# Sixteen 32x32 products in the expert combine, and a new order around two norms and two projections

## The chip, the cores and the metric

The kernel runs on one core of one Trainium2 chip. The metric is device time in microseconds (us), median of several executions; lower is better. All arithmetic that counts is 4-byte floating point. Where the program wants the accuracy of full precision from the faster rounded form (fp32r), it splits both operands into a high and a low part and makes three matmuls of one product.

## The reference, cut to what matters

Two blocks on 512 tokens of width 1024. The change touches only the first:

```
mod = silu(c) @ w_ada + b_ada                  # 6 vectors of 1024: shift1, scale1, gate1, shift2, scale2, gate2
hn = rmsnorm(x, norm1_g) * (1 + scale1) + shift1
... = split(hn @ w_in)                         # heads of two attentions, gates ga, gb
merged = sigmoid(ga) * (ya @ w_proj_a) + sigmoid(gb) * (yb @ w_proj_b)
x = x + gate1 * (merged @ w_out)
hn2 = rmsnorm(x, norm2_g) * (1 + scale2) + shift2
qh = hn2 @ w_q ; s = qh . sub_keys             # 8 heads x 2 halves x 128 keys
eidx, g = the 16 best of 16 x 16 sums, softmax # 8 heads x 16 experts for each token
pre = hn2 . u[eidx] ; coef = g * gelu(pre)
f = sum over the 128 of coef * v[eidx]         # the combine
x = x + gate2 * f
```

The second block (attention with forget gates, pooling, a feed-forward of width 2816) follows; `u` and `v` are tables of 16384 rows of 1024.

## The kernel before, in words

Everything is written out by hand for each engine: the order of the work is the order of the code in the blocks `sync`, `tensor`, `scalar`, `vector` and `gpsimd`, and semaphores tie them together (`ready(n)` waits until n+1 events have been told, `free(n, depth)` until n+1-depth have). Activations lie transposed, channels on the partitions. A dense tile is 1024 input rows by 128 output columns of weights, 512 KB, and comes through a ring of four slots from SyncE's queue (`refill`, L623 and L662). ScalarE rounds it (`high`, L1323), VectorE takes the remainder (`low`, L1915), TensorE makes 8 x 3 matmuls of 512 columns (`product`, L688 to L690; `dense`) and the result goes to one of eight PSUM banks.

**The first norm.** SyncE loads `w_ada` in 48 tiles of 512 KB through six slots (L617): six, then `x` (2 MB), then ten more, then the first four weight tiles. VectorE makes one dot product for each (`ada_tile`, L1897). Tiles 0 to 7 are shift1, 8 to 15 scale1. When all sixteen are done it adds the bias (L1910), makes the gain, splits weight tile 0, and then goes over the eight channel tiles: `hn` (L1894), the rounded part on ScalarE (L1332), the low part `hn_low` (L1894). TensorE takes weight tile 0 as these come (a wait for each k in `dense`), and tile 1 after it.

**The projections.** After the attention, eight tiles of both `w_proj` (each 2 x 4 x 3 matmuls, ya first and yb second, one bank each: 0,1 and 2,3 in turn), then eight of `w_out` (banks 0 and 1). VectorE gates and adds each pair (L2079 to L2082), splits the sum (`merged_high`, `merged_low`), and tells `dense_dve`. TensorE waits for all of ya, yb and the gates before the first `w_proj` tile and for the last merged tile before the first `w_out` tile.

**The second norm and the queries.** The same as the first norm, with `w_q` tiles: `query(0)`, then `query(1)`, `key_scores(0)`, `query(2)`, `key_scores(1)`, `token_rows(0)`, and so on (L904 to L934). `choose(0)` on VectorE begins when the key scores of tiles 0 and 1 have been copied out, and ends with the first 16 expert numbers, which release GpSimd's first gather.

**Experts.** For each of 4 x 8 x 16 = 512 rows n, GpSimd issues an indirect DMA (`gather`, L1867) that brings, for each of 128 tokens, one row of u beside one row of v, 8 KB, 1 MB in all, into one of eight slots. VectorE multiplies the u half with the token's row (`dots`, L1897), ScalarE makes gelu and weight (L1512, L1518) and scales a folded unit matrix with it into `diag` (L1526), and TensorE adds the v halves (`combine`, L947), two rows at a time. A slot may be filled again when its combine has been made. Between the combines stand, by a fixed table of ticks, the remaining queries and the whole second block for the first half of the tokens (`block2(0)`); the second half (`block2(1)`) comes after the last combine.

The combine cuts the 128 tokens in two halves, so that four 64x64 quarters of the array are in use:

```
for a in range(2):
    for odd in range(2):
        s = (n + odd) % SLOT
        for t in range(2):
            k = slice(HALF * t, HALF * t + HALF)
            b = t ^ odd
            last = mm(bank(4 + 2 * odd + a)[HALF * b:HALF * b + HALF, :], diag[k, s, :],
                      rows[k, s, D + a * 512:D + (a + 1) * 512], start=c == 0, stop=c == P - 2)
```

Even rows n add into banks 4 and 5, odd ones into 6 and 7 with the halves crossed. `turn` brings both back to channels on partitions, with the unit matrix and with one whose halves are crossed (L963, L964).

## Time and profile before

| | |
|---|---|
| time, median of 3 runs | 2453.24 us (2450.24 to 2456.2) |
| the profiled execution's own time | 2461.37 us |
| its span in the profile | 2459.6 us |
[...]
| busy: PE, PEld, DVE, ACT, POOL | 84%, 50%, 58%, 41%, 24% |
| combine (L947): records, busy, mean | 4096, 632.0 us, 744 ns |
| gathers (L1867): issues; queue's bytes | 512; 542.25 MB |
| read from HBM | 707.56 MB, 289 GB/s over the span |

PE is TensorE's matmuls, PEld its weight loads, DVE VectorE, ACT ScalarE, POOL GpSimd, SP SyncE; SPq and DVEq are sequencers. A 4-byte (f32) product has two records in the trace, an fp32r one has one. Busy time of PE overlaps with itself, since matmuls are pipelined and their ends are modelled; the start of the next instruction is the better measure. "x16" is a count of records, and what stands in brackets is the idle time before and who ended it.

### The profile page before, as it was taken

The numbers are of one execution on the slowest core, as the hardware profiler recorded it, in microseconds if no ns is written. First come the engines' busy times: TensorE is split into PE (matmuls) and PEld (weight loads), VectorE is DVE, ScalarE is ACT, GpSimd is POOL, SyncE is SP. The second block draws the span as 40 slices with busy tenths as digits, with TensorE's granted clock in tenths as the row PEclk, the third lists the DMA queues.
The fourth block names the chain that finished last, engine by engine and source line by source line (L and its number), as shares of the span: only waits on it lengthen the run. The fifth ranks groups of instructions, "written<-read, shape, count | busy, mean of one in ns | idle before, by whom it ended". The sixth has DMA issues, their size and how long they took to land.

```text
span 2459.6 us, 29836 instructions
## 1 busy us (share of the span) xinstructions
PE 2063.2 (84%) x10672; PEld 1239.6 (50%) x10672; DVE 1427.6 (58%) x3242; ACT 1008.1 (41%) x2400; POOL 593.7 (24%) x570
## 2 busy tenths in 40 slices
PE   5999999999878765655656798889999987899999
PEld 3877557776534321111112363345666653677887
DVE  7742764453777677777777858774433433222554
ACT  3123435523434333333334566854444312353443
POOL 0000000000344444445444324433333331000000
PEclk9999999999988877878687899889999998999999
DMA  8821002132899999999999999999999997313655
GB/s 324 311 78 69 1 18 67 62 95 76 327 420 420 420 420 418 414 421 418 413 420 396 390 382 383 394 388 419 418 418 418 418 418 319 113 52 103 181 180 170
DMA packets 123585, 711.59 MB, mean 289 GB/s; under 512 B 14593, under 2 KB 15745, under 8 KB 57649
## 3 DMA queue, kind: packets, MB, share of 16 engines
q0 software_dynamic: 74608, 542.25, 53.7%
q1 hardware_dynamic: 48592, 167.33, 19.4%
q8 instruction: 81, 1.33, 0.2%
q14 instruction: 64, 0.52, 0.1%
q10 hardware_dynamic: 240, 0.16, 0.0%
HBM read 707.56 MB, written 2.13 MB: 289 GB/s over the span
## 4 chain that ended last, share of the span: by engine, by line
PE 57%; DMA 25%; DVE 7%; ACT 6%; issue 3%; POOL 2%; ACTq 0%; SPq 0%; DVEq 0%
DMA arena<-experts,eidx 24%; PE psum L947 10%; PE psum L688 8%; PE psum L689 8%; PE psum L690 8%; PE psum L1259 5%; DVE arena L1897 4%; POOL arena L1867 2%; PE psum L1237 2%; PE psum L1114 2%; PE psum L1064 2%; PE psum L800 1%; ACT sq L1526 1%; PE psum L776 1%; ACT arena L1518 1%
## 5 line engine op out<-in xcount | busy, mean ns | idle before, releaser
L947 PE MATMUL psum<-arena,sq 64*64 64x512 f32 x4096 | 632.0, 744 | 321.5 <-ACT sq L1526 311.8
L1897 DVE CUSTOM_DVE_ANT_0 arena<-arena 128x1024 f32<-128x1024 f32 x560 | 679.0, 1224 | 358.9 <-DMA arena<-experts,eidx 325.2
L1867 POOL DMA_INDIRECT arena<-experts,eidx x512 | 577.5, 1128 | 957.7 <-PE psum L947 773.7
L947 PEld LDWEIGHTS psum<-arena,sq 64*64 64x64 f32 x4096 | 153.8, 155 | 707.3 <-ACT sq L1526 472.3
L1512 ACT ACTIVATE arena<-arena 128x2 f32<-128x2 f32 x256 | 52.1, 203 | 718.1 <-DVE arena L1897 706.3
L688 PE MATMUL psum<-hn_high,w_high 128*128 128x512 f32 (+1 forms) x432 | 179.0, 414 | 14.7 <-DVE hn_low L1894 13.3
L689 PE MATMUL psum<-hn_low,w_high 128*128 128x512 f32 (+1 forms) x432 | 173.8, 402 | 0.0
L690 PE MATMUL psum<-hn_high,ring_low 128*128 128x512 f32 (+1 forms) x432 | 172.5, 399 | 0.0
L1259 PE MATMUL psum<-n_t,ring 128*128 128x256 f32 x704 | 161.7, 384 | 0.6 <-issue 0.6
L1526 ACT ACTIVATE sq<-sq,arena 128x64 f32<-128x64 f32 x512 | 150.3, 340 | 24.1 <-ACT arena L1518 0.4
L1259 PEld LDWEIGHTS psum<-n_t,ring 128*128 128x128 f32 x704 | 130.7, 190 | 45.7 <-issue 29.4
L1915 DVE TENSOR_TENSOR ring_low<-ring,w_high 128x1024 fp32r<-128x1024 f32 x74 | 90.4, 1224 | 77.2 <-ACT w_high L1323 70.7
L1323 ACT ACTIVATE w_high<-ring 128x1024 fp32r<-128x1024 f32 x74 | 77.6, 1052 | 133.6 <-PE psum L690 127.4
L2205 DVE TENSOR_TENSOR ring_low<-ring,last_high 128x1024 fp32r<-128x1024 f32 x66 | 80.7, 1225 | 82.9 <-ACT last_high L1550 82.2
L1518 ACT ACTIVATE arena<-arena 128x1 f32<-128x1 f32 x512 | 122.9, 287 | 10.6 <-ACT arena L1512 0.4
L688 PEld LDWEIGHTS psum<-hn_high,w_high 128*128 128x128 f32 (+1 forms) x432 | 82.2, 190 | 60.5 <-issue 33.8
L1550 ACT ACTIVATE last_high<-ring 128x1024 fp32r<-128x1024 f32 x66 | 69.8, 1060 | 82.1 <-DMA ring<-w_stream 82.1
L1512 ACT ACT_TABLE_LOAD x75 | 96.2, 1283 | 6.0 <-ACT hn_rest L1785 3.7
L690 PEld LDWEIGHTS psum<-hn_high,ring_low 128*128 128x128 f32 (+1 forms) x432 | 82.3, 190 | 20.1
L689 PEld LDWEIGHTS psum<-hn_low,w_high 128*128 128x128 f32 (+1 forms) x432 | 82.6, 191 | 17.4
L1856 POOL TENSOR_SCALAR_AFFINE_SELECT arena<-arena 128x128 f32<-128x128 f32 x32 | 9.4, 295 | 272.0 <-DVE arena L1894 271.6
L688 PE MATMUL psum<-last_high,n_high 128*128 128x512 f32 (+1 forms) x192 | 72.6, 378 | 1.2 <-DVE n_low L2218 1.1
(316 smaller groups left out, 3150.5 us busy)
## 6 DMA issues: line engine op xcount, KB each, us to landing
ring<-w_stream SPq DMA_DIRECT2D x262, 512.0 KB
arena<-w_ada SPq DMA_DIRECT2D x48, 512.0 KB, 6.4
arena<-experts,eidx POOLq DMA_INDIRECT x512
arena<-cum_rows POOLq DMA_DIRECT2D x1, 2112.0 KB, 10.3
x<-xT SPq DMA_DIRECT2D x1, 2048.0 KB, 15.2
arena<-rel_rows POOLq DMA_DIRECT2D x1, 2048.0 KB, 15.2
arena<-sub_keys POOLq DMA_DIRECT2D x1, 1024.0 KB, 6.3
outT<-hn_rest SPq DMA_DIRECT2D x8, 128.0 KB, 10.1
```

The lines of the kernel that those rows point to most:

```text
L688: mm(out, a[0], b[0], start=start, stop=False)
L689: mm(out, a[0], b[1], start=False, stop=False)
L690: return mm(out, a[1], b[0], start=False, stop=stop)
L947: last = mm(bank(4 + 2 * odd + a)[HALF * b:HALF * b + HALF, :], diag[k, s, :], rows[k, s, D + a * 512:D + (a + 1) * 512], start=c == 0, st ...
L1259: last = mm(bank(b, PAIR), w[:, k, :], n_t[:, k, 0:PAIR], start=k == 0, stop=k == KT - 1)
L1512: steps(op(pre[:, s:s + 2], pre[:, s:s + 2], ACT.Gelu))
L1518: steps(op(coef[:, s + c:s + c + 1], pre[:, s + c:s + c + 1], ACT.Copy, scale=wgt[:, n // P % 2, k:k + 1]))
L1526: op(diag[:, s + c, :], ident_pair, ACT.Copy, scale=coef[:, s + c:s + c + 1]).then_inc(diag_done.sem, 1)
L1867: nc.gpsimd.indirect_dma_start(rows[:, s, :], None, experts, bass.IndirectOffsetOnAxis(ap=eidx[:, n // P % 2, n % P:n % P + 1], axis=0)).t ...
L1897: return V.tensor_tensor_reduce(out=out, in0=a, in1=b, scale=1.0, scalar=0.0 if op1 == ALU.add else -TAKEN, op0=op0, op1=op1, accum_out=accum)
L1915: V.tensor_tensor(ring_low[:, n % SLOTS, :], ring[:, n % SLOTS, :], rounded(n).bitcast(f32), ALU.subtract)\
L2205: V.tensor_tensor(ring_low[:, n % SLOTS, :], ring[:, n % SLOTS, :], last_high[:, n % SLOTS, :].bitcast(f32), ALU.subtract).then_inc(w_spli ...
```

## The change

1. **Combine.** The tokens are cut in quarters of 32. For each half a of the columns and each of two rows (odd), four products of 32x32x512 go to one bank, quarter t of the tokens to quarter t ^ (2*odd + a) of the partitions, so that the sixteen products of one combine use sixteen different 32x32 tiles. `diag` and the folded unit matrix become 32 wide, the latter made with three additions for one, and `turn` uses matrices that undo the crossing.
2. **First norm.** `w_ada` is loaded in the order scale1, shift1, the rest. SyncE issues three tiles, `x`, five tiles, weight tiles 0 and 1, eight tiles, weight tiles 2 and 3. VectorE makes the gain after eight tiles, and then for each k one more dot product, one bias addition of one column, `hn`, and `hn_low` of k-2, with the splits of weight tiles 0 and 1 at k = 1 and 2. A small step on the attention's bias rows moves behind the second product tile.
3. **Both norms.** `first_two` takes weight tiles 0 and 1 together: tile 1 runs three k behind tile 0 in the other bank. After the second norm ScalarE copies both, and `key_scores` 0 and 1 come before `query(2)` and `token_rows(0)`.
4. **Projections.** yb goes ahead of ya; tile 0 waits for ya k by k, only tile 1 for the gates' copies; banks (2,3) and (0,1) in turn. The first `w_out` tile waits for the merged tiles k by k, the others for the bank. The loops are written out.

```diff
-            for n in range(ADA_SLOTS):
+            for n in range(3):
                 ada_load(n)
             eng.dma_start(x[:, :, META:], xT.rearrange("(k p) t -> p k t", p=P)).then_inc(x_loaded, 16)
-            for n in range(ADA_SLOTS, ADA_FIRST):
+            for n in range(3, KT):
                 ada_load(n)
-            for n in range(SLOTS):
+            for n in range(2):
+                refill(n)
+            for n in range(KT, ADA_FIRST):
+                ada_load(n)
+            for n in range(2, SLOTS):
                 refill(n)
...
+            def first_two(t0, norm_part):
+
+                ws = [None, None]
+                for step in range(KT + 3):
+                    for c in range(2):
+                        k = step - 3 * c
+                        if 0 <= k < KT:
+                            if k == 0:
+                                ws[c] = tile(t0, c)
+                            pe.wait_ge(hn_ready.sem, hn_ready.ready(norm_part * KT + k))
+                            last = product(bank(c), part(ws[c], ALL, k), part(rhs, ALL, k), k == 0, k == KT - 1)
+                            if k == KT - 1:
+                                last.then_inc(tile_done.sem, 1)
...
-            pe.wait_ge(y_taken.sem, y_taken.ready(HP - 1))
             pe.wait_ge(yb_taken.sem, yb_taken.ready(HP - 1))
-            pe.wait_ge(dense_act.sem, dense_act.ready(A_WQ - 1))
...
+            pe.wait_ge(s_taken.sem, s_taken.ready(2 * S - 1))
+            for m in range(KT):
+                w = tile(S_PROJ, m)
+                if m == 1:
+                    pe.wait_ge(dense_act.sem, dense_act.ready(A_WQ - 1))
+                pe.wait_ge(dense_dve.sem, dense_dve.free(V_PROJ + m, 2))
+                for e in (1, 0):
+                    for k in range(HP):
+                        if m == 0 and e == 0:
+                            pe.wait_ge(y_taken.sem, y_taken.ready(k))
...
+                for k in range(KT):
+                    if m == 0:
+                        pe.wait_ge(dense_dve.sem, dense_dve.ready(V_PROJ + k))
...
-            query(0)
-            for j in range(LEAD - 1):
+            for j in range(2):
+                pe.wait_ge(dense_act.sem, dense_act.free(A_WQ + j, 2))
+            first_two(S_WQ, 1)
+            key_scores(0)
+            key_scores(1)
+            query(2)
+            token_rows(0)
+            for j in range(2, LEAD - 1):
                 query(j + 1)
                 key_scores(j)
...
-                        for t in range(2):
-                            k = slice(HALF * t, HALF * t + HALF)
-                            b = t ^ odd
-                            last = mm(bank(4 + 2 * odd + a)[HALF * b:HALF * b + HALF, :], diag[k, s, :],
+                        for t in range(4):
+                            k = slice(QUART * t, QUART * t + QUART)
+                            b = t ^ (2 * odd + a)
+                            last = mm(bank(4 + 2 * odd + a)[QUART * b:QUART * b + QUART, :], diag[k, s, :],
                                       rows[k, s, D + a * 512:D + (a + 1) * 512], start=c == 0, stop=c == P - 2)
...
-            for n in range(ADA_FIRST):
+            for n in range(KT):
                 ada_tile(n)
             dve.wait_ge(vec_loaded, 16)
-            ada_bias(0, ADA_FIRST)
...
+            for k in range(KT + 2):
+                if k < KT:
+                    if k + 1 < KT:
+                        ada_tile(KT + k + 1)
+                    dve.wait_ge(ada_used.sem, ada_used.ready(KT + k))
+                    steps(V.tensor_tensor(mod[:, k:k + 1], mod[:, k:k + 1], vec[:, B_ADA + k:B_ADA + k + 1], ALU.add))
+                    if k == 0:
+                        root(0)
+                if k in (1, 2):
+                    low(k - 1)
```

How the order changes on the engines (line numbers of each kernel's own file):

VectorE in the first norm. Before, behind the sixteenth dot product (the rows named `ISA`):

```order
L1910 TENSOR_TENSOR mod<-mod,vec 128x16 [waits ada_used,vec_loaded]
L1894 SCALAR_TENSOR_TENSOR gain<-mod,vec 128x8 [waits dve_step]
L1915 TENSOR_TENSOR ring_low<-ring,w_high 128x1024 [waits w_rounded]
L1894 SCALAR_TENSOR_TENSOR hn<-x,gain,rstd 128x512 [waits root_ready,dve_step]
L1894 SCALAR_TENSOR_TENSOR hn<-x,gain,rstd 128x512 x2
L1894 SCALAR_TENSOR_TENSOR hn_low<-hn,mod,hn_high 128x512 [waits high_ready]
```

Now, around k = 2, with six dot products still to come:

```order
L1942 ISA arena,mod<-arena 128x1024 [waits ada_ready5]
L1942 ISA mod 128x1
L2004 TENSOR_TENSOR mod<-mod,vec 128x1 [waits ada_used]
L1961 TENSOR_TENSOR ring_low<-ring,w_high 128x1024 [waits w_rounded]
L1939 SCALAR_TENSOR_TENSOR hn_low<-hn,mod,hn_high 128x512 [waits high_ready]
L1939 SCALAR_TENSOR_TENSOR hn<-x,gain,rstd 128x512 [waits dve_step]
L1942 ISA arena,mod<-arena 128x1024 [waits ada_ready0]
```

The dot products of shift1 have moved from before the norm's loop into it.

ScalarE behind the second norm. `arena<-psum 128x512` is a query's copy, `128x4x128` the copy of key scores, `128x1024` the token rows, `w_high` the rounding of a weight tile. Before:

```order
L1482 ACTIVATE arena<-psum 128x512 [waits key_done,tile_done]
L1323 ACTIVATE w_high<-ring 128x1024 [waits tile_done,ring_ready0]
L1482 ACTIVATE arena<-psum 128x512 [waits key_done,tile_done]
L1323 ACTIVATE w_high<-ring 128x1024 [waits tile_done,ring_ready1]
L1488 ACTIVATE arena<-psum 128x4x128 [waits key_done]
L1482 ACTIVATE arena<-psum 128x512 [waits key_done,tile_done]
L1323 ACTIVATE w_high<-ring 128x1024 [waits tile_done,ring_ready2]
L1488 ACTIVATE arena<-psum 128x4x128 [waits key_done]
L1496 ACTIVATE arena<-psum 128x1024 [waits htok_done]
```

Now:

```order
L1522 ACTIVATE arena<-psum 128x512 [waits key_done,tile_done] x2
L1363 ACTIVATE w_high<-ring 128x1024 [waits tile_done,ring_ready0]
L1528 ACTIVATE arena<-psum 128x4x128 [waits key_done] x2
L1363 ACTIVATE w_high<-ring 128x1024 [waits tile_done,ring_ready1]
L1522 ACTIVATE arena<-psum 128x512 [waits key_done,tile_done]
L1363 ACTIVATE w_high<-ring 128x1024 [waits tile_done,ring_ready2]
L1536 ACTIVATE arena<-psum 128x1024 [waits htok_done]
```

Both copies of key scores have moved ahead of the third query's copy; the rounding of the third weight tile stands behind the copies of both queries.

TensorE at the first combine, before and now:

```order
L947 MATMUL psum<-arena,sq 64x512 [waits diag_done,acc_done]
L947 MATMUL psum<-arena,sq 64x512 x7
```

```order
L986 MATMUL psum<-arena,sq 32x512 [waits diag_done,acc_done]
L986 MATMUL psum<-arena,sq 32x512 x15
```

Sixteen products stand where eight stood, behind the same waits.

## Rows read from the trace of the kernel before

**Rows 1.** The page's 40 slices: granted clock and GB/s.

```profile
PEclk9999999999988877878687899889999998999999
GB/s 324 311 78 69 1 18 67 62 95 76 327 420 420 420 420 418 414 421 418 413 420 396 390 382 383 394 388 419 418 418 418 418 418 319 113 52 103 181 180 170
```

**Rows 2.** Busy time by stage: length, PE, PEld, DVE, ACT, POOL, clock, DMA, GB/s.

```profile
640.00:1380.00 740.00, 476.15 (x2744) 165.60 (x2748) 558.18 (x1496) 284.06 (x866) 331.25 (x286) 0.80 1.01 417
1380.00:1640.00 260.00, 233.86 (x1217) 105.88 (x1210) 184.84 (x517) 169.79 (x418) 98.74 (x87) 0.88 0.96 381
1640.00:1900.00 260.00, 253.81 (x1436) 166.12 (x1439) 118.97 (x223) 118.76 (x278) 88.06 (x82) 0.99 1.02 418
1900.00:2100.00 200.00, 169.04 (x952) 103.96 (x944) 75.37 (x131) 50.74 (x161) 51.74 (x50) 0.96 0.89 368
```

**Rows 3.** Chain of waits in 1380 to 1640 us, summed by line.

```profile
by line: PE psum L947 19.7%; PE psum L1114 17.8%; DVE arena L1897 10.7%; DMA arena<-experts,eidx 8.4%; PE psum L1130 5.7%; ACT L1685 3.9%; issue 3.6%; ACT arena L1518 3.2%; ACT sq L1526 3.1%; ACT L1512 2.0%; ACT hn_rest L1685 2.0%; PE psum 
```

**Rows 4.** Timeline of the first norm: start us, us, engine line op.

```profile
19.59 1.28 ACT L1342 ACT_TABLE_LOAD   x1 [12.56 <-DMA x<-xT]
...
20.89 1.23 DVE L1897 CUSTOM_DVE_ANT_0 arena<-arena 128x1024 f32<-128x1024 f32 x1 [5.43 <-DMA arena<-w_ada]
...
31.65 0.63 ACT L1339 ACTIVATE rstd<-rstd 128x512 f32<-128x512 f32 x1
...
35.91 2.07 DVE L1894 SCALAR_TENSOR_TENSOR hn<-x,gain,rstd 128x512 f32<-128x512 f32 x3
...
44.52 2.07 DVE L1894 SCALAR_TENSOR_TENSOR hn_low<-hn,mod,hn_high 128x512 fp32r<-128x512 f32 x3
...
53.71 0.33 SPq L623 DMA_DIRECT2D ring<-w_stream  x1
...
59.27 0.33 SPq L623 DMA_DIRECT2D ring<-w_stream  x1
```

**Rows 5.** Timeline, and one window, where the projections begin.

```profile
477.44 1.09 PE L860 MATMUL psum<-arena 128*64 128x128 f32 x16 [1.23 <-ACT arena L1450]
...
480.41 0.79 PE L688 MATMUL psum<-ya_high,w_high 128*128 128x512 f32 x1 [1.87 <-DVEq L605]
...
480.40:486.00 5.60, 5.59 (x13) 4.44 (x14) 0.00 (x0) 2.01 (x2) 0.00 (x0) 0.50 0.00 0
```

**Rows 6.** The same where the output projection begins.

```profile
531.34 0.79 PE L688 MATMUL psum<-merged_high,w_high 128*128 128x512 f32 x1 [3.42 <-DVEq L605]
...
531.30:537.20 5.90, 5.86 (x14) 4.60 (x15) 1.23 (x1) 0.00 (x0) 0.00 (x0) 0.50 0.36 149
```

**Rows 7.** Timeline from the second norm to the first gather.

```profile
590.83 0.76 PE L688 MATMUL psum<-hn_high,w_high 128*128 128x512 f32 x1 [4.31 <-DVE hn_low L1894]
...
605.13 1.05 PE L913 MATMUL psum<-arena 128*128 128x128 f32 x8
...
613.85 0.49 DVE L2106 MAX8 arena<-arena 128x8 f32<-128x128 f32 x2 [11.28 <-ACT arena L1488]
...
626.91 1.02 POOL L1867 DMA_INDIRECT arena<-experts,eidx  x1 [98.13 <-DVEq L605]
```

**Rows 8.** One combine: timeline, two 30 ns windows, and pieces of the chain.

```profile
1705.37 1.95 PE L947 MATMUL psum<-arena,sq 64*64 64x512 f32 x16
...
1705.37:1705.40 0.03, 0.03 (x4) 0.03 (x4) 1.00 0.00 0
...
1705.85:1705.88 0.03, 0.03 (x8) 0.03 (x4) 1.00 0.00 0
...
1396.02 3.69 PE psum L947 x16
...
1406.04 1.88 PE psum L947 x16
```

**Rows 9.** Chain of waits where the gathers end: start us, us, what.

```profile
2063.02 16.86 DMA arena<-experts,eidx
...
2082.62 3.76 PE psum L947 x16
```

More of the change, by code:

```diff
@@ L54 @@
 SQ0, MS = [0, 8], [0, 1]
+PROJ_BANK, OUT_BANK = (2, 0), (2, 0)
 PAIR = 2 * P
@@ L1951, in low_part @@
                 steps(V.tensor_tensor(low, raw, high.bitcast(f32), ALU.subtract))
-            root(0)
-            norm(0, META, gain1, 0, mod[:, 0:KT])
-            low(1)
-            dve.wait_ge(rel_done.sem, rel_done.ready(0))
-            steps(V.tensor_scalar(rel_row, bank(4, REL)[0:NH, :], -1.0, None, ALU.mult))
-            tell(dve, steps, rel_copied)
+            for k in range(KT + 2):
[8 more added lines that the diff above has]
+                    low(k - 1)
+                if k >= 2:
+                    c = k - 2
+                    dve.wait_ge(high_ready.sem, high_ready.ready(c))
+                    stt(hn_low[:, c, META:], hn[:, c, META:], mod[:, c:c + 1], hn_high[:, c, META:].bitcast(f32),
+                        ALU.add, ALU.subtract).then_inc(hn_ready.sem, 1)
+                if k < KT:
+                    steps.wait()
+                    stt(hn[:, k, META:], x[:, k, META:], gain1[:, k:k + 1], rstd[:, META:], ALU.mult, ALU.mult)\
+                        .then_inc(normed.sem, 1)
             def qk_out(m):
@@ L1967, in _ @@
                 low(m + 2)
+                if m == 1:
+                    dve.wait_ge(rel_done.sem, rel_done.ready(0))
+                    steps(V.tensor_scalar(rel_row, bank(4, REL)[0:NH, :], -1.0, None, ALU.mult))
+                    tell(dve, steps, rel_copied)
                 for n in range(ADA_FIRST + 2 * m, min(ADA_FIRST + 2 * m + 2, ADA)):
@@ L2420, in _ @@
             low(S_WQ + 7)
-            steps(V.tensor_tensor(ident_pair, ident[:, 0:HALF], ident[:, HALF:P], ALU.add))
+            steps(V.tensor_tensor(ident_quart, ident[:, 0:QUART], ident[:, QUART:2 * QUART], ALU.add))
+            for t in range(2, 4):
+                steps.wait()
+                steps(V.tensor_tensor(ident_quart, ident_quart, ident[:, QUART * t:QUART * (t + 1)], ALU.add))
             tell(dve, steps, pair_ready)
```

81 lines of the change are left out of this document (45 added, 36 removed).

## The prediction

> **What bounds the kernel now.** I read the page's slices first, then the stages, then the chain of waits inside the stage that stood out, and last the timeline at each place that the diff touches. The slices [rows 1] show three parts. After the loads at the start and up to about 627 us little is moved (under 113 GB/s): this is the attention, a chain through TensorE. From there to about 2076 us the gathers run, and for most of it GB/s stands at 413 to 421, whatever the engines do: that is the ceiling of this kernel's transfers, so this stage is set by bytes, not by the combine. The rest is the second half of block 2, on TensorE. The stages [rows 2] say the same: DMA 1.01 to 1.02 of full in two of them, but 0.96 and 381 GB/s in 1380 to 1640 us. There the transfers waited for something, and the chain [rows 3] names the combine, L947, first, with 19.7% of 260 us, then the products of block 2, then dot products and ScalarE. So what counts is how much sooner the first gather is issued, how much of the dip between slices 21 and 26 is filled, and what lies behind the last transfer. TensorE time saved while the queue is full is worth nothing.
>
> **The change part by part**, against the profiled execution (2461.4 us; its median of runs is 2453.2, and I take the difference over to that).
>
> *First norm: 0 us (2 less to 3 more).* `x` now comes behind three tiles and not six. The last tile ahead of `x` is used by 13 us, and VectorE sat idle 5.43 us until the first tile behind `x` came [rows 4]; 6 MB had landed by 19.6 us, so three tiles less ahead of it (1.5 MB) are some 4 us. Mean square and root took 12.7 us from `x` (19.59 to 32.28), so they would end at 28. But VectorE was the bound: before, its last `hn_low` ended at 46.6 (44.52 + 2.07), sixteen dot products, two splits and sixteen passes of 0.66 after it began. Now seven of the dot products (1.28 each) stand in the norm's loop, with eight small additions of 0.2. From 28 us: k = 0 0.7; k = 1 3.4; k = 2 4.1; four steps of 2.9; the rest 3: 22.8, so 50.8 us. TensorE then has four products of tile 1 left (2.8 us), since `first_two` has done the others: 53.6. Before, tile 1 ended at 53.7, by the ring's refill that waits for it [rows 4]. The scale parts come sooner, and the sum is nil. The upper end is for TensorE staying at its lower clock, as it may with products coming in pairs every 2.9 us: four products at 0.43 per matmul instead of 0.23.
>
> *Start of the projections: 3.5 us less (1.9 to 4.5).* TensorE ended the last values at 478.5, stood idle 1.87 us for the last split of ya and then ran 13 matmuls at the lower clock, 0.43 us each [rows 5]. At the full clock one is 0.23 (a tile is 24 of them, and two refills are 5.56 us apart [rows 4]). Now yb's 12 matmuls need no wait and last 2.8 us, longer than the 1.9 of the split. That gives back the idle time and up to 13 x 0.2 = 2.6 us. I take somewhat more than half of the 2.6, because the short matmuls ahead may let the clock fall anyway.
>
> *First `w_out` tile: 6.2 us less (3.4 to 6.4).* Here 3.42 us of idle time and 14 slow matmuls [rows 6]. The last merged tile is ready about 3.6 us after the last `w_proj` product; seven of the eight k of the first `w_out` tile last 7 x 3 x 0.23 = 4.8 us and need only older ones. The wait is covered and the clock has no reason to fall: 3.4 + 14 x 0.2. What is late next is the split of the second `w_out` tile, needed 5.6 us later, and VectorE has it 1.3 us after the merged tile.
>
> *Second norm to first gather: 2.5 us less (0 to 6.7).* Two tiles ran from 590.83 to 605.13 with waits in between [rows 7]; together they end near 604.2. The key scores of both follow, and `choose(0)` starts near 607.1 instead of 613.85. It took 13 us to the first gather at 626.91, three splits in it. Now it is held up by the later of these: tile 2 starts at 607.1 (its split waits for both queries), ends at 612.7, the token rows take 1.8, tile 3 ends at 620.1; copy 0.6, rounding 1.05, split 1.23 and the rest of `choose` 1.2 give 624.2. So most of the 6.7 us goes into a new wait on tile 3. Two extra additions for the folded unit matrix (0.2 each) lie behind it, while eight gathers of 2.5 us are under way.
>
> *Combine in the gather stage: 15 us less (0 to 27).* One combine now is 16 records, four starting within one 30 ns window and four more at 1705.85, 0.48 after them; the chain's pieces are 1.88 us at the full clock and 3.69 at the lower [rows 8]: four rounds of four tiles, 0.43 to 0.47 each. After the change 32 records stand on sixteen tiles: two rounds, 0.94, and 0.1 for the starts, so about 1.05 us, and 1.9 cold. No row shows sixteen tiles at once; the other end is four at a time, 8 rounds, 3.6 us. I take 1.05, since the row's four tiles cost no more than one matmul would. In 1380 to 1640 the combine is 19.7% = 51 us of the chain; 44% of that is 22.6 us. What can be won at most is the missing transfer: slices 21 to 26 against 419 GB/s lack 23 + 29 + 37 + 36 + 25 + 31 = 181, times 61.5 us, over 419: 26.6 us. ScalarE and VectorE stand beside in the chain and take over where the combine gets short; two thirds of 22.6 is 15. In 1640 to 1900 TensorE is busy 254 of 260 us [rows 2] and still worth nothing, since the transfers run at 418.
> [...]
>
> *End: 1.8 us less.* The last transfer releases dots, ScalarE and one cold combine of 3.76 [rows 9], now 1.9.
>
> Sum: 0 + 3.5 + 6.2 + 2.5 + 15 + 1.8 = 29.0 us. The profiled execution would be 2432, the median **2424 us**.
>
> **The rivals.**
> *A, the combine pays nothing on the path* (22%). Either 32 instructions with 32 weight loads take as long as 16 did, or ScalarE and the dots hold the dip where it is, or the shorter combines leave TensorE at its lower clock. For it: clock 0.80 and 0.88 in the two stages [rows 2], and that most of the chain in the dip isn't the combine. Against: 19.7%. Only the front counts: 12 less, 2441.
> *B, the dip is filled* (14%). Cold combines are twice as dear, and the pieces of the chain that start after a combine move up with it. 12.2 + 26.6 + 1.8 = 41 less, 2412.
> *C, slower* (6%): the array feeds only four such tiles at once, or the four row groups that write one bank go one after the other. Both give 3.6 us per combine, 1.7 more. 43 and 41 combines (half of x87 and x82 [rows 2]) are 143 us of TensorE; 26 and 6 are free there, so 111 come out, and 11 more in 1900 to 2100 (25 combines against 31 free); in 640 to 1380 there is room. 122 - 12 = 110 more, 2563. It decides from a combine of 2.4 us, where 84 x 0.52 passes the 32 free and the 12 won. Against it: in the first four records of a combine two row halves write the same bank, on different partitions, and start within 30 ns [rows 8].
> [...]
> *D, the first norm or a wait that I have misread costs over 5 us* (3%): about 2430 to 2440 still.
>
> **How the numbers follow.** Forecast 55% (20 to 38 less), A 22%, B 14%, C 6%, D 3%. Range 2409 to 2443: B's and A's bounds with the unknowns of the front, without C. Under 0.2%, 4.9 us, a measurement can't tell this kernel from no change. Faster by more 90%, within 3% (A with the front at its low ends), slower 7%.
>
> **What would show it.** Right: TensorE starting on yb straight after the last values, no idle time ahead of the first `w_out` product, first gather about 12 us earlier, a combine of 1.0 to 1.1 us with starts of sixteen close together, slices 21 to 26 above 400 GB/s. Wrong: combines over 2.4 us or TensorE at 260 of 260 in the later gather stage; a dip as deep as before, with ScalarE and dots in its chain (A); or first-norm tile 1 ending after 56 us.

## The result, and the profile after

| | before | after |
|---|---|---|
| median (range), us | 2454.65 (2450.24 to 2461.56), 7 runs | 2437.67 (2431.3 to 2442.79), 7 runs |
| ratio, 95% interval | | 0.9917 (0.99 to 0.9934), some 20 us less |
| the profiled execution's own time; span | 2461.37; 2459.6 | 2432.89; 2430.9 |
| mean granted TensorE clock, as a share of full speed | 0.912 | 0.838 |
| combine: records, busy | 4096, 632.0 us | 8192, 419.2 us |

The kernel is 0.8% faster; forecast were 2424 us and a range of 2409 to 2443. The two profiled executions differ by 28.5 us, almost the forecast 29, but the medians by 17 and the ratio says 20. The closeness to 29 is luck, as the last part of the account below works out, and that gap is the main thing to explain.

The page's slices of granted clock and GB/s after, to be read beside rows 1 (slices are counted from 0, here and in the prediction, so 21 to 26 are 396 to 388 before and 406 to 401 now):

```profile
PEclk8999999999878655555555797688999997999999
GB/s 304 330 88 70 1 9 70 64 111 70 367 420 419 420 420 417 419 416 418 417 419 406 400 418 392 415 401 419 417 418 417 417 418 303 114 53 108 185 178 170
```

The stages after [rows 2] (length, PE, PEld, DVE, ACT, POOL, clock, DMA, GB/s), and the start of the chain of waits in 1380 to 1640 us, summed by line [rows 3]:

```profile
640.00:1380.00 740.00, 370.29 (x5080) 126.30 (x5062) 555.79 (x1480) 277.85 (x866) 379.32 (x290) 0.60 1.01 417
1380.00:1640.00 260.00, 233.73 (x2070) 115.98 (x2072) 192.44 (x534) 171.39 (x435) 101.90 (x90) 0.82 0.99 404
1640.00:1900.00 260.00, 224.41 (x2048) 154.31 (x2016) 113.04 (x200) 118.18 (x272) 86.65 (x80) 0.95 1.02 418
```

```profile
by line: DMA arena<-experts,eidx 16.0%; PE psum L986 11.8%; PE psum L1154 8.9%; DVE arena L1942 6.8%; PE psum L1170 6.5%; PE psum L1277 4.0%; issue 4.0%; ACT L1557 3.9%; ACT sq L1571 3.5%; ACT arena L1563 3.4%; ACT L1630 3.0%; ACT L1730 3.0
```

TensorE has 106 us less to do in the first stage and 29 less in the third, and the transfers run at 417 and 418 GB/s there, as before: that time bought nothing. Only the dip, the stretch of 1380 to 1640 us, changed: from 381 to 404 GB/s. In its chain the combine (L986) fell from 19.7% to 11.8%; the gathers themselves now stand first with 16.0%.

The chain at four combines, after, at the lower and at the full clock (0.50 and 1.00 in the windows of the first two) [rows 8], and the last transfer and combine (0.50) [rows 9]:

```profile
1381.47 2.02 PE psum L986 x32
...
1391.07 1.07 PE psum L986 x32
...
2036.35 16.57 DMA arena<-experts,eidx
...
2055.61 2.20 PE psum L986 x32
```

Stretches after: 26 and 27 products where 13 and 14 stood [rows 5, 6], and 0.1 us of a combine (the x counts every record that overlaps the window; here sixteen of the combine and the last of the group ahead of it):

```profile
478.50:484.20 5.70, 5.70 (x26) 4.62 (x25) 1.38 (x2) 3.97 (x3) 0.00 (x0) 1.00 0.01 3
523.20:529.10 5.90, 5.90 (x27) 4.77 (x26) 4.43 (x7) 2.35 (x2) 0.56 (x1) 1.00 0.74 267
...
1700.50:1700.60 0.10, 0.10 (x17) 0.10 (x31) 0.00 (x0) 0.10 (x1) 0.00 (x0) 1.00 1.47 614
```

The timeline ahead of the gathers, after [rows 4 to 7]:

```profile
15.33 1.28 ACT L1382 ACT_TABLE_LOAD   x1 [8.25 <-DMA x<-xT]
...
27.73 0.63 ACT L1379 ACTIVATE rstd<-rstd 128x512 f32<-128x512 f32 x1
...
53.51 0.50 PE L696 MATMUL psum<-hn_high,w_high 128*128 128x512 f32 x1
...
478.53 0.50 PE L696 MATMUL psum<-yb_high,w_high 128*128 128x512 f32 x1
...
523.24 0.39 PE L696 MATMUL psum<-merged_high,w_high 128*128 128x512 f32 x1
...
576.99 2.08 DVE L1939 SCALAR_TENSOR_TENSOR hn<-x,gain,rstd 128x512 f32<-128x512 f32 x3 [0.39 <-ACT rstd L1379]
...
593.53 2.01 PE L948 MATMUL psum<-arena 128*128 128x128 f32 x16
...
596.45 0.48 DVE L2169 MAX8 arena<-arena 128x8 f32<-128x128 f32 x2
...
613.77 1.02 POOL L1912 DMA_INDIRECT arena<-experts,eidx  x1 [89.51 <-DVEq L609]
```

The first product of each projection has no idle time ahead of it, and the first gather is issued at 613.77 instead of 626.91.

### The profile page after: what moved, and what is told of

Same layout as the page of the kernel before. It is cut to its first block, busy times and chain, and to the rows that moved or that the text cites. A ratio compares the mean times of both kernels' runs of the same rounds, so it can differ in the third digit from the quotient of the medians.

```text
span 2430.9 us, 38013 instructions
## 1 busy us (share of the span) xinstructions
PE 1887.3 (78%) x14768; PEld 1178.9 (48%) x14768; DVE 1427.8 (59%) x3252; ACT 993.5 (41%) x2400; POOL 639.3 (26%) x570
## 3 DMA queue, kind: packets, MB, share of 16 engines
q8 instruction: 114, 1.87, 0.3%
## 4 chain that ended last, share of the span: by engine, by line
PE 49%; DMA 31%; ACT 7%; DVE 6%; POOL 3%; issue 3%; ACTq 0%; SPq 0%; DVEq 0%
DMA arena<-experts,eidx 31%; PE psum L696 8%; PE psum L697 8%; PE psum L698 8%; PE psum L986 6%; DVE arena L1942 4%; POOL arena L1912 3%; PE psum L1277 2%; PE psum L1104 2%; PE psum L827 2%; ACT sq L1571 1%; ACT arena L1563 1%; PE psum L803 1%; PE psum L1299 1%; PE psum L1154 1%
## 5 line engine op out<-in xcount | busy, mean ns | idle before, releaser
L1912 POOL DMA_INDIRECT arena<-experts,eidx x512 | 623.2, 1217 | 889.8 <-PE psum L986 717.0
L986 PE MATMUL psum<-arena,sq 32*32 32x512 f32 x8192 | 419.2, 855 | 474.0 <-ACT sq L1571 458.3
L986 PEld LDWEIGHTS psum<-arena,sq 32*32 32x32 f32 x8192 | 68.4, 121 | 717.2 <-ACT sq L1571 672.4
L1299 PEld LDWEIGHTS psum<-n_t,ring 128*128 128x128 f32 x704 | 132.9, 193 | 48.9 <-issue 30.7
L1571 ACT ACTIVATE sq<-sq,arena 128x32 f32<-128x32 f32 x512 | 136.7, 313 | 24.1 <-ACT arena L1563 0.4
```

The costliest lines, as they stand in the source:

```text
L986: last = mm(bank(4 + 2 * odd + a)[QUART * b:QUART * b + QUART, :], diag[k, s, :], rows[k, s, D + a * 512:D + (a + 1) * 512], start=c == 0, ...
L1299: last = mm(bank(b, PAIR), w[:, k, :], n_t[:, k, 0:PAIR], start=k == 0, stop=k == KT - 1)
L1571: op(diag[:, s + c, :], ident_quart, ACT.Copy, scale=coef[:, s + c:s + c + 1]).then_inc(diag_done.sem, 1)
L1912: nc.gpsimd.indirect_dma_start(rows[:, s, :], None, experts, bass.IndirectOffsetOnAxis(ap=eidx[:, n // P % 2, n % P:n % P + 1], axis=0)).t ...
```

## Experiments

Each run stands against runs of the kernel before on its own chip. The positions in the second table are read from the one profiled execution of each kernel.

| run | what it is | median, us | ratio to before (95%) |
|---|---|---|---|
| e4_null | before, unaltered | 2457.40 | 0.9996 (0.9981 to 1.0011) |
| e1_front | changed, with the 64x64 combine | 2448.25 | 0.9954 (0.9938 to 0.997) |
| e2_combine | before, with the new combine | 2446.77 | 0.9965 (0.995 to 0.9981) |
| e3_whole | changed, unaltered | 2436.07 | 0.9924 (0.9902 to 0.9946) |
| e5_four_tiles | changed, four tiles in use | 2560.60 | 1.0436 (1.0412 to 1.046) |
| e6_eight_tiles | changed, eight tiles in use | 2448.02 | 0.9975 (0.9963 to 0.9987) |
| e7_ticks | changed, ticks spread otherwise | 2434.72 | 0.9931 (0.9911 to 0.995) |
| e8_sooner | changed, splits moved | 2436.94 | 0.9935 (0.9916 to 0.9954) |
| e9_old_norm | changed, first norm of before | 2435.73 | 0.9927 (0.991 to 0.9945) |
| e10_old_projections | changed, projections of before | 2447.90 | 0.9962 (0.9947 to 0.9978) |
| e11_sooner_again | e8, mended | 2431.23 | 0.9903 (0.9887 to 0.9919) |
| e12c_sooner_ticks | e11 with the ticks of e7 | 2429.63 | 0.9906 (0.9885 to 0.9928) |

| profile | end of the values | from there to the first gather | to the last landing | to the end |
|---|---|---|---|---|
| before | 478.5 | 148.4 | 1453.0 | 379.7 |
| e4_null | 476.2 | 146.6 | 1447.9 | 378.8 |
| e1_front | 478.2 | 135.3 | 1449.9 | 384.6 |
| e6_eight_tiles | 479.1 | 135.3 | 1449.9 | 377.8 |
| e2_combine | 478.3 | 148.4 | 1439.3 | 378.2 |
| after | 478.5 | 135.2 | 1439.2 | 378.0 |
| e3_whole | 477.6 | 135.5 | 1438.8 | 379.8 |
| e9_old_norm | 478.1 | 135.1 | 1439.0 | 378.0 |
| e10_old_projections | 479.0 | 146.0 | 1439.1 | 381.2 |
| e5_four_tiles | 478.7 | 135.3 | 1563.8 | 379.6 |
| e7_ticks | 478.4 | 135.2 | 1437.1 | 379.8 |
| e8_sooner | 480.4 | 130.3 | 1443.0 | 379.8 |
| e11_sooner_again | 484.3 | 130.0 | 1438.1 | 381.2 |
| e12c_sooner_ticks | 478.7 | 130.0 | 1439.6 | 383.0 |

The values are the attention's last products. The third column of numbers, from the first gather's issue to the last landing, is called the gather stage. The end of the values is the start of the first `w_proj` product, less the 1.87 us of idle time where the old projections stand (before, e4, e2, e10).

**The two halves of the change, apart and together.** In e1 the combine and its turn are those of before, in e2 they alone are new:

```diff
-                        for t in range(4):
-                            k = slice(QUART * t, QUART * t + QUART)
-                            b = t ^ (2 * odd + a)
+                        for t in range(2):
+                            k = slice(HALF * t, HALF * t + HALF)
+                            b = t ^ odd
```

> The changed kernel with the combine of before (four 64x64 products for each half of the columns, turned with the matrix of before); everything else of the change stays. My theory: the parts ahead of the gathers bring the first gather 12 to 13 us forward (near 614 us of the span) and nothing is given back later, so the ratio to the kernel before is 0.9943 to 0.9955, some 11 to 14 us less. Rival: the earlier start is partly lost in the dip of the transfers, because the cold combines then meet other work: 5 to 9 us less. A second rival is that the combine alone brought the whole gain: 0 to 3 us less.

> The kernel before with the new combine alone (sixteen 32x32 products for each half, the quarter-wide unit matrix and its turn). My theory: one combine takes 1.05 us at the full clock and 2.0 at the lower, the first gather stays at 627 us, the dip of 1380 to 1640 us is filled in part, and the last combine is 1.5 us shorter: 5 to 17 us less, ratio 0.993 to 0.998, by what the changed kernel showed in its median against its profile. Rival A: the shorter combine is worth nothing in the gather stage because ScalarE, the dots and the transfers set its length: 0 to 3 us less.

> The changed kernel once more, unaltered. If the parts are independent its gain is the sum of the two runs beside it: some 20 us less, ratio 0.9905 to 0.9935. Its profile tells whether the place of the last landing (2053 us in the first profile) holds from one execution to the next or wanders by 5 us or more; the first gather should stand at 613.8 within 0.5 us.

> The kernel before, unaltered, as a measure of what two equal kernels differ by: ratio 0.999 to 1.001. Its profile has the first gather at 626.9 within 0.5 us; if the wandering of the time lies in the gather stage, the last landing differs from 2079.9 us by up to 6 us, and the dip of 1380 to 1640 us moves less or more than the 381 GB/s of the first profile.

Measured: 11.3 us less for the front (0.0046 of 2457), 8.6 for the combine, together 19.9; the whole change gives 18.7 here and 20.4 in the first comparison. Within the intervals, some 4 us to either side of each, nothing speaks against independent parts. The rival that one half brought the whole gain falls, and so does rival A: the interval of e2 leaves out 1. Two of the expectations on single positions missed: e4's first gather stood at 622.8 and not 626.9, its last landing 9.2 us ahead of 2079.9 where up to 6 was expected, and e3's first gather stood at 613.1 and not 613.8. Both come in part from the end of the values, which moves from one execution to the next; so the table counts from there. The second table says more than the times do. The way from the values to the first gather is 146.6 to 148.4 us with the old front and 135.2 to 135.5 with the new one, and the gather stage is 1447.9 to 1453.0 with eight tiles or four 64x64 ones (four profiles, mean 1450.2) and 1438.8 to 1439.3 with sixteen (five profiles with nothing else changed behind the first gather, mean 1439.1): 11.1 us. e1's 1449.9 also shows that nothing of its earlier start was lost in the dip. e1's own end was 5 us longer than that of the kernel before (384.6 against 379.7), for which see the last section.

**How many tiles a combine needs.** The sixteen products stay, with the same bytes and the same number of instructions; only the quarter of the partitions that each goes to is changed, so that they share eight or four tiles of the array:

```diff
-                            b = t ^ (2 * odd + a)
+                            b = t ^ (2 * odd)
```

```diff
-                            b = t ^ (2 * odd + a)
+                            b = t
```

> The changed kernel with quarter t of the tokens always sent to quarter t of the partitions, so that the sixteen products of a half share the four tiles on the array's diagonal; the turn uses the plain unit matrix. Same number of instructions and bytes. My theory (the number of different tiles sets the time of a combine, not the size of the product): 8 rounds of four, 3.6 us per combine at the full clock, TensorE becomes the bound of the later gather stage, and the time comes near the 2563 us that the prediction gave for this price (2500 to 2600). Rival: the gain comes from smaller weight loads or smaller products, and this kernel is no slower than the changed one by more than 5 us, with a combine under 1.9 us.

> The changed kernel with quarter t sent to quarter t for even rows and to t ^ 2 for odd ones, in both halves of the columns: eight different tiles. My theory: 4 rounds, 1.9 us per combine at the full clock, 3.7 at the lower, as the four 64x64 products of before took, and so the time of the kernel that has only the new front (2448 us; 0.9945 to 0.997 of before). Rival: twice as many instructions and weight loads as with 64x64 cost something of their own: slower than the front-only kernel by 3 us or more.

Pieces of the chain of waits of e5 at the full clock, and its stages (same columns as above):

```profile
1647.41 3.57 PE psum L986 x32
...
1658.91 5.38 PE psum L1277 x24
```

```profile
1380.00:1640.00 260.00, 255.70 (x1697) 107.50 (x1693) 163.42 (x455) 159.14 (x382) 85.07 (x76) 0.99 0.90 339
1640.00:1900.00 260.00, 258.85 (x1743) 141.09 (x1735) 109.36 (x226) 95.72 (x241) 77.74 (x71) 1.00 0.93 356
```

A combine of e6 in its timeline and in its chain, and then 0.05 us inside a combine of e5, e6 and the changed kernel, with the records in flight as the first x:

```profile
1699.92 1.95 PE L986 MATMUL psum<-arena,sq 32*32 32x512 f32 x32
...
1699.99 1.88 PE psum L986 x32
```

```profile
1647.50:1647.55 0.05, 0.05 (x4) 0.00 (x0) 0.00 (x0) 0.00 (x0) 0.00 (x0) 1.00 1.93 819
...
1700.10:1700.15 0.05, 0.05 (x8) 0.00 (x0) 0.00 (x0) 0.05 (x1) 0.00 (x0) 1.00 1.57 656
...
1700.55:1700.60 0.05, 0.05 (x16) 0.05 (x31) 0.00 (x0) 0.05 (x1) 0.00 (x0) 1.00 2.55 1065
```

Four, eight and sixteen records run at once. By the chain a combine takes 3.57 us with four tiles, 1.88 with eight, 1.07 with sixteen: the number of rounds, 8, 4 or 2, times 0.45 to 0.54 us. In these runs the size of a product does not enter: eight tiles of 32x32 take what four of 64x64 took (1.88 in both, 1.95 in both timelines). Whether twice the instructions and weight loads cost something besides is less clear. The medians of e6 and of the front-only kernel are 2448.02 and 2448.25, and both gather stages 1449.9 us; but by the ratios, each against runs of before on its own chip, e6 is 5 us slower (0.9975 against 0.9954, intervals that overlap by 0.0007), and 0.9975 lies outside the 0.9945 to 0.997 expected. The traces show no place for such a cost. With four tiles TensorE is busy 258.85 of 260 us, the transfers fall to 356 GB/s, and the time is 2560.6: the prediction had worked out 2563 for a combine of 3.6 us. So its account of a stage that TensorE sets holds at that price; the turning point that it placed at 2.4 us was not measured.

**The first norm and the projections, each undone alone.** e9 takes back the order of `w_ada`, SyncE's queue, the first `first_two` and VectorE's loop:

```diff
-ADA_ORDER = [*range(8, 16), *range(8), *range(16, ADA)]
+ADA_ORDER = [*range(ADA)]
...
-            first_two(S_QK, 0)
-            for m in range(2, 4):
+            for m in range(4):
                 w = tile(S_QK, m)
                 pe.wait_ge(dense_dve.sem, dense_dve.free(m, 2))
-                dense(bank(m % 2), w, rhs).then_inc(tile_done.sem, 1)
+                dense(bank(m % 2), w, rhs, 0 if m == 0 else None).then_inc(tile_done.sem, 1)
```

> The changed kernel with the first norm of before: w_ada in its own order behind six tiles, all sixteen dot products ahead of the norm, weight tile 1 after tile 0. Second norm, projections and combine stay changed. My theory (the prediction's first term, 0 us): tile 1 ends at 53 to 54 us either way, everything behind it keeps its place, and the time is that of the changed kernel within 2 us. Rival: the new order brings a gain that the clock of the next stretch hides or shows: 2 to 4 us more than the changed kernel, with the first product of the projections that much later.

e10 takes back TensorE's order of the projections:

```diff
-            pe.wait_ge(s_taken.sem, s_taken.ready(2 * S - 1))
-            for m in range(KT):
-                w = tile(S_PROJ, m)
+            pe.wait_ge(dense_act.sem, dense_act.ready(A_WQ - 1))
+            with pe.Fori(0, 2) as q:
+                for j in range(4):
+                    w = tile(S_PROJ, j, q, 4)
...
-            pe.wait_ge(dense_dve.sem, dense_dve.ready(V_PROJ + KT - 2))
+            pe.wait_ge(dense_dve.sem, dense_dve.ready(V_OUT - 1))
```

> The changed kernel with TensorE's projections of before: ya ahead of yb, one wait for all of ya, yb and the gates ahead of the first tile, one wait for the last merged tile ahead of w_out, banks as before. My theory: the idle 1.87 and 3.42 us and the 13 and 14 matmuls at the lower clock come back, so the first product behind the second norm and the first gather are 9 to 11 us later than in the changed kernel, and so is the end: ratio 0.9955 to 0.9975 of before. Rival: a later start of the gathers is partly made good in the dip: 3 to 6 us more than the changed kernel.

The new first norm is worth nothing that can be measured: 2435.73 us without it, ratio 0.9927, and the values end at 478.1 against 478.5 and 477.6 with it. The new projections are worth what was forecast for them: without them the first gather is 10.8 us later (146.0 against 135.2), the ratio 0.9962 against 0.9917 to 0.9927, some 9 us. The idle times come back at the same places, in e10's timeline:

```profile
480.88 0.79 PE L696 MATMUL psum<-ya_high,w_high 128*128 128x512 f32 x1 [1.87 <-DVEq L609]
...
531.85 0.80 PE L696 MATMUL psum<-merged_high,w_high 128*128 128x512 f32 x1 [3.42 <-DVEq L609]
```

Nothing of the later start was made good in the dip (1439.1 us of gather stage), so the rival of e10 falls. The clock was 0.50 from 480.88 to 486.40 and from 531.85 to 537.80 us, with 13 and 14 matmuls as in the kernel before.

**What is left in the dip.** e7 spreads the second block's ticks thinner where the dip is:

```diff
-    return 0 if n < FIRST_TICK else 1 + (n % 4 == 0)
+    if n < FIRST_TICK:
+        return 0
+    return 1 + (n % 8 == 0 if n < FIRST_TICK + 116 else n % 8 in (0, 3, 6))
```

> The changed kernel with the second block's ticks spread otherwise: 1.125 per row for the first 116 rows from the first tick on, then 1.375 (before 1.25 throughout). The dip of the transfers lies in the first stretch, and TensorE has 35 us free of 260 in the second. My theory: what is left of the dip (slices 21 to 26 lack some 80 GB/s-slices, about 12 us) is work of block 2 on TensorE and ScalarE between two combines, so a thinner spread fills a part: 2 to 7 us less than the changed kernel, slices 21 to 26 over 408 on average. Rival: the stalls come from single long groups of products between two combines, which stay as long as they were: within 2 us, and the dips only move. Second rival: the later stage becomes too dense and loses what the first wins.

Slices 21 to 26 of e7:

```profile
GB/s 306 329 87 70 1 9 70 63 111 70 366 420 419 420 420 419 417 417 417 420 417 410 406 408 419 407 397 419 417 418 417 417 418 290 114 53 107 186 178 170
```

They lack 67 against 82 in the changed kernel, the gather stage is 1.7 to 2.2 us shorter, and the time is the same within its interval: the theory of 2 to 7 us falls. Not even the 67 can be put down to the ticks, since e10 lacks 68 with the old ones. The rival had the time right. Its reason, that the stalls come from long groups of products between two combines and only move, is argued and not shown: in e7's chain of 1380 to 1640 us the dot products (L1944) hold 16.5% and the first group of block 2 (L1156) 12.0%. In the changed kernel's chain such a group looks so:

```profile
1462.93 2.02 PE psum L986 x32
1464.95 7.71 PE psum L1170 x12
1472.66 1.07 PE psum L986 x32
1473.73 3.73 PE psum L1170 x8
1477.47 1.07 PE psum L986 x32
```

Between the combines that end at 1464.95 and begin at 1472.66 stand 7.71 us of block 2 (L1170), more than the 5 us in which two rows are transferred (2.1 MB at 417 GB/s). The combine between two such groups is 1.07 us, and a shorter one would gain little there.

**A version that starts the gathers sooner.** Before the first gather the changed kernel's VectorE waits twice for ScalarE to round a weight tile that the first choice of experts does not need. ScalarE rounds the one behind its copy of query tile 2, the other behind that of tile 3:

```profile
604.02 1.23 DVE L1961 TENSOR_TENSOR ring_low<-ring,w_high 128x1024 fp32r<-128x1024 f32 x1 [2.80 <-ACT w_high L1363]
...
611.39 1.23 DVE L1961 TENSOR_TENSOR ring_low<-ring,w_high 128x1024 fp32r<-128x1024 f32 x1 [1.50 <-ACT w_high L1363]
```

e8 moves these splits behind the steps that lead to the expert numbers, and brings the first pair's dot products, `diagonals(0)` and `combine(0)` forward:

```diff
-                    if part_of in (0, 4, 9):
-                        low(S_WQ + 3 + (0, 4, 9).index(part_of))
+                    if part_of in (0, 7, 10):
+                        low(S_WQ + 3 + (0, 7, 10).index(part_of))
             low(S_WQ + 6)
-            low(S_WQ + 7)
...
+            dots(0)
+            dots(1)
+            low(S_WQ + 7)
```

> The changed kernel with two splits of weight tiles moved out of the first choice of experts (the second from before the best-of-256 search to the place before the one-hot step, the third to behind the told expert numbers), and the first pair's dot products, weights and combine ahead of the split of the eighth query tile and of the key scores 4 and 5. The trace shows VectorE idle for 2.80 and 1.50 us at those splits. My theory: first gather at 608 to 609 us of the span instead of 613.8, first combine at 623 to 626 instead of 630, and 4 to 5 us less than the changed kernel. Rival: the gathers start sooner but the queue then stands still for the first combines, or query tiles 5 and 6 come late and push block 2: 0 to 2 us less.

The start was won (130.3 us from the values to the gather, 5.0 less) and lost again (gather stage 1443.0, 4 more); the time is the rival's, not the theory's. Some 1.8 us of the loss lie in 640 to 680 us, where the changed kernel ran at 418 and 422 GB/s; where the other 2 went was not found. e8:

```profile
640.00:660.00 20.00, 17.61 (x200) 10.19 (x200) 19.14 (x54) 8.68 (x27) 6.50 (x6) 0.69 1.00 405
660.00:680.00 20.00, 12.20 (x132) 6.50 (x120) 15.04 (x42) 6.62 (x21) 11.92 (x9) 0.66 0.99 398
```

VectorE is nearly full in the first of them (19.14 of 20 us). TensorE is no less busy from 650 to 660 us (10.00 of 10), so which of the two held the transfers was not separated. The second choice of experts had been left until after the splits of tiles 6 and 7, for which VectorE stood idle 4.88 and 2.83 us. e11 runs six of its twelve parts in that time:

```diff
-            low(S_WQ + 6)
...
-            low(S_WQ + 7)
-            choosing = {}
+            choosing = choose(PLAN[0][0][0])
+            for p in range(6):
+                next(choosing)
+                if p == 1:
+                    low(S_WQ + 6)
...
+                if n == 2:
+                    low(S_WQ + 7)
```

> The kernel with the moved splits, mended where its trace showed new waits: the dot products of the first pair ahead of the split of query tile 6, six of the twelve parts of the second choice of experts run while VectorE stood idle at 615 to 627 us, the split of tile 7 behind the dot products of the second pair. My theory: what the earlier start won (3.2 us) was lost at 640 to 680 us, where VectorE was the bound (19.1 of 20 us busy) and the transfers fell to 405 and 398 GB/s; with the second choice begun 8 us sooner these stay at 415 to 421, and the time is 3 to 4 us under the changed kernel. Rival: another wait of the first hundred microseconds takes its place (key scores, the splits of tiles 6 and 7): less than 1.5 us.

> The mended kernel with the moved splits and, besides, the other spread of the second block's ticks (1.125 per row for 116 rows, then 1.375). My theory: the moved splits take 4 us off the changed kernel again (ratio 0.989 to 0.9915 of before), the ticks 0 to 2 us more, since with them alone the time stayed within the noise and the last landing came 1 to 2 us sooner: ratio 0.9885 to 0.991. Rival: the first result of the moved splits was luck, and this kernel is within 1.5 us of the changed one (0.9915 to 0.9935).

The same stretch of e11:

```profile
640.00:660.00 20.00, 13.87 (x168) 7.83 (x168) 16.15 (x44) 5.88 (x20) 7.91 (x9) 0.91 1.01 419
660.00:680.00 20.00, 10.30 (x116) 5.01 (x116) 15.69 (x44) 9.26 (x26) 7.87 (x7) 0.66 1.01 421
```

The dip at 640 us is gone and the 5 us are kept (130.0 us from the values to the gather, gather stages of 1438.1 and 1439.6). e11 and e12c stand at 0.9903 and 0.9906, the kernels with the changed start of the gathers and sixteen tiles (after, e3, e9) at 0.9917, 0.9924 and 0.9927: 0.0018 of 2455, 4 to 5 us, or 4 to 8 by medians. The intervals of single runs overlap, but two different kernels with this edit both came out below all three without it. The ticks add nothing that can be seen. So the mended version beats the kernel before clearly and the changed kernel probably: 2430 to 2431 us against 2452 to 2457 and 2436 to 2438.

## Why the prediction was right, and where it was off

*First norm, 0 us: the number right, the way to it partly by luck.* `x` landed at 15.33 instead of 19.59 and the root ended at 28.36 (27.73 + 0.63), 28 in the working. Tile 2 starts at 53.51, so tile 1 ended at 53.5; 53.6 was forecast, 53.7 is before. The dot products in the norm's loop took back what the earlier `x` gave, and e9 confirms the nil. But the working had VectorE end at 50.8 and TensorE four products (2.8 us) behind it. The trace has VectorE's last `hn_low` at 48.9, since a step of the loop took 2.5 us and not 2.9, and TensorE still 4.6 us of work behind that:

```profile
42.84 0.79 PE L696 MATMUL psum<-hn_high,w_high 128*128 128x512 f32 x1 [0.89 <-DVE hn_low L1939]
...
47.30 1.62 DVE L1939 SCALAR_TENSOR_TENSOR hn_low<-hn,mod,hn_high 128x512 fp32r<-128x512 f32 x2
```

From 42.84 on TensorE's products run without a gap, up to 45.57 still at the lower clock (0.50, with 0.43 us from one matmul to the next), then 0.23 us apart. So at the end TensorE was the bound and not VectorE, and two errors of some 1.9 us cancel.

*Projections, 3.5 and 6.2: the mechanism right, the first term a little small.* By the two traces 4.7, just above its bound of 4.5, and 6.3: from the end of the values to the first `w_out` product less its idle time 49.4 us before (1.87 + 47.5) and 44.7 after; then 3.42 of idle time and 56.6 us to the second norm's `hn` before, 53.8 after. Of the first term the clock's part was taken too small: all thirteen slow products vanished, not "somewhat more than half". Where TensorE came straight from the values' short products the clock was 1.00 (the window from 478.50 us above); behind an idle time of 1.87 or 3.42 us, in the kernel before and again in e10, it was 0.50.

*Second norm to first gather, 2.5: right.* 38.96 us before (587.95 to 626.91), 36.78 after: 2.2. As forecast, most of the head start (the choice began 6.4 us sooner) went into new waits, which show as VectorE's idle 2.80 us behind tile 2 and 1.50 behind tile 3; the working had only the latter. What it missed besides is that these waits were not the gather's own but those of two splits with no hurry; e8 and e11 took them out.

*Combine in the gather stage, 15: the price of a combine right, what it is worth too high.* 1.07 us at the full clock, 2.02 at the lower; 1.05 and 1.9 were forecast. Sixteen records are in flight at once (the window from 1700.55 us above), four row groups of them on one PSUM bank, each on its own 32 partitions, and e5 shows what a combine of four at a time would have cost, 3.57 us. So rival C fell with its mechanism, not by luck. Neither a limit of four tiles at once nor row groups that go one after the other on a bank would fit 1.07 us for 32 records.

The term of 15 us is the step that failed in size. It was "two thirds of 22.6", where 22.6 is what the shorter combine takes off the chain in 1380 to 1640 us, and 26.6, what slices 21 to 26 lacked, was the most that could be won. The chain did get shorter by nearly that: 19.7% of 260 us before, 11.8% now, 20.5 us. But the gather stage gave only 11.1 us, half of 22.6 and not two thirds; the factor had no row behind it. The dip says the same. The execution shown had the deepest one of the four profiles with a 1.9 us combine: the others (e4, e1, e6) lack 151, 161 and 151 slice-GB/s, 22.1, 23.5 and 22.0 us by the same working, a mean of 23.5. After, the slices lack 82, 79, 77, 82 and 68 (after, e3, e2, e9, e10), 11.3 us. So the dip was half filled, by 12.2 us. In the chain of that stretch the gathers themselves rose from 8.4% to 16.0%, and block 2's products (L1154, L1170 and L1277) hold 19.4%, in groups of up to 7.7 us; what share of the remaining dip each of them makes, no run separates. Neither A (nothing) nor B (all of it) holds.

*End, 1.8: not seen in the total.* The last combine went from 3.76 to 2.20, 1.6 us, but what lies behind the last landing is 378 to 385 us in all profiles, old and new, so in the total it does not show.

*Carrying the sum over to the median.* The forecast of 2424 was 13.4 us under the median of 2437.7. The sum was made against one execution at 2461.4, some 7 us over the medians of before, which are 2452 to 2457; after's profiled execution was at 2432.9, 4.8 under its median. These two differ by 13.2 us up to the first gather, 13.8 in the gather stage and 1.7 behind it, 28.7 together, which looks like the 29.0 of the sum. That is luck: by the means of all profiles it is 12.5 (147.8 to 135.3) and 11.1, 23.6 us, and nothing certain at the end. Of the 13.4, the terms are 5.4 (29.0 less 23.6, chiefly the combine's and the end's); 3.2 lie between the profiles' 23.6 and the ratio's 20.4; 3.4 between the ratio and the difference of the medians, 17.0; and 1.4 because the median of before was 2453.2 in three runs and 2454.7 in seven. The last three are of the size by which the same kernel's runs move, and what part of them is chance stays open.

The range of 2409 to 2443 held, but the time alone would not have told the forecast from rival A: 17 to 20 less lies at or below the forecast's own 20 to 38, and 2437.7 is nearer to A's 2441 than to 2424. What tells them apart is e2 and the gather stages.

## What to carry to other kernels

The packed small products of this kernel cost rounds, 8, 4 and 2 of 0.45 to 0.54 us (e5, e6 and the changed kernel): count how often each tile of the array is used, and choose the mapping of inputs to output partitions so that no two products share one. In a stage that the transfers set, read the worth of a faster engine from what the transfers lack and from what else stands between two of its steps, and take both from more than one execution: one pair of profiles gave 13.8 us where the means of four and of five gave 11.1. And when a start is moved forward, follow the second and third item too: e8 won 5 us at the first gather and lost 4 of them in the gather stage, nearly half of that within 70 us.

## What was not expected of the hardware

**The granted clock sets much of the spread.** The attention's work is the same in all these kernels, and yet the end of the values wandered from 476.2 to 484.3 us. One stretch, 210 to 300 us, of e4, the changed kernel and e11, TensorE alone (length, PE, clock, DMA, GB/s):

```profile
210.00:300.00 90.00, 85.89 (x451) 1.00 0.08 28
```

```profile
210.00:300.00 90.00, 86.31 (x439) 0.96 0.07 26
```

```profile
210.00:300.00 90.00, 86.31 (x419) 0.91 0.10 34
```

451, 439 and 419 products fit into the stretch, and the values ended at 476.2, 478.5 and 484.3 us: more or less time at the lower level (in windows of 3 us e4 shows 1.00 in all thirty, e11 0.50 to 0.54 in five), and up to 8 us between kernels that do nearly the same work up to there. e3, e8 and e11, which are the same up to there and had nearly the same clocks before 210 us (0.88, 1.00 and 0.93 in the three 70 us of each), line up: 1.00, 0.96 and 0.91 in this stretch, and the values end at 477.6, 480.4 and 484.3 us. The timed runs agree: of the 23 of before beside e1, the shortest (2450.3 us) had a mean clock of 0.920 and the longest (2466.1) 0.908. What makes one execution fall to the lower level and another not, no run shows. Behind the last landing it is the same: e1's end was 384.6 us, and there the clock stood at 0.50 and 0.67 where the changed kernel's was 0.99 and 1.00 (in the 10 us before it was the other way round, 0.82 and 0.50). e1, then after, from 10 us behind the last landing on:

```profile
2073.30:2083.30 10.00, 6.91 (x26) 0.50 0.00 0
2083.30:2093.30 10.00, 7.84 (x22) 0.67 0.00 1
```

```profile
2062.90:2072.90 10.00, 6.23 (x35) 0.99 0.00 0
2072.90:2082.90 10.00, 6.82 (x31) 1.00 0.01 2
```

**A faster engine was granted a lower clock, and in the first stage it cost nothing.** With combines half as long the mean granted clock fell from 0.912 to 0.838, 0.80 to 0.60 in the first stage of the gathers, where TensorE is now busy 370 of 740 us and was 476. With four tiles (e5) it stood at 0.99 and 1.00 from 1380 to 1900 us. Read alone, 0.60 looks like a loss; the transfers ran at 417 GB/s in that stage, before and after. In the dip, where the combine does count, the lower clock makes it 2.02 us and not 1.07.
